# Fifteen small transfers move from SyncE's issue queue to ScalarE's in a two-block transformer kernel

## The reference

```
mod = silu(c) @ w_ada + b_ada                 # 2048 -> 12288, six parts of 2048
h   = rms_norm(x, g_attn_pre) * (1 + scale_a) + shift_a
proj = h @ w_in                               # 2048 -> 5456
... rope with positions; lam = exp(sum(lambda_q1*lambda_k1)) - exp(sum(lambda_q2*lambda_k2)) + lam_init
... differential attention, indexed sparse attention, @ w_o, gated feed-forward (w_gate, w_up, w_down)
... second block: rms_norm(x, pre_norm_g_2), @ w_in_2, latent attention with rope(positions_2),
    a gated convolution with conv_w_2, @ w_o_mla_2, @ w_o_conv_2, @ w_out_2
```

## Time and profile before

| what | value |
|---|---|
| median of 3 runs | 2428.31 us (2427.94 to 2430.77) |
| profiled execution, its own time | 2428.22 us |
| its span | 2426.9 us |
| PE busy / weight loads | 94% / 77% of the span |
| DVE, ACT busy | 58%, 44% |
| mean granted clock of PE | 0.978 of full |
| moved by the transfers | 505.69 MB, mean 208 GB/s |

### The profile page before, as it was taken

The page is one execution under the profiler, slowest core; times in us unless marked ns, Lnnn a source line. Parts: engine busy times, 40 slices in busy tenths (PEclk is TensorE's granted clock), DMA queues, the critical chain, the costliest instruction groups (busy, mean ns, idle before and its releaser), DMA issues.

```text
span 2426.9 us, 26309 instructions
## 1 busy us (share of the span) xinstructions
PE 2291.2 (94%) x10768; PEld 1861.1 (77%) x10768; DVE 1399.5 (58%) x1903; ACT 1062.3 (44%) x1469; POOL 0.7 (0%) x5
## 2 busy tenths in 40 slices
PE   4898989798999999999999999999999999999998
PEld 2676667676878888888887878788888888888886
DVE  1459898686666464454555555454544554554554
ACT  2333534444434444444444555555444444444443
POOL 0000000000000000000000000000000000000000
PEclk7999999899999999999999999999999999999999
DMA  7888678484776575556554644444555556556553
GB/s 296 333 314 306 216 262 285 153 306 166 247 273 243 192 259 191 191 191 191 191 189 143 210 157 154 153 152 152 185 196 192 188 184 197 183 186 194 187 190 139
DMA packets 255455, 505.69 MB, mean 208 GB/s; under 512 B 9077, under 2 KB 19662, under 8 KB 254182
## 3 DMA queue, kind: packets, MB, share of 16 engines
q1 hardware_dynamic: 255334, 504.00, 61.6%
HBM read 499.77 MB, written 4.19 MB: 208 GB/s over the span
## 4 chain that ended last, share of the span: by engine, by line
PE 82%; DVE 10%; ACT 3%; DMA 3%; issue 2%; SPq 0%; DVEq 0%; ACTq 0%
PE bank L566 26%; PE bank L568 25%; PE bank L567 25%; DVE wlo L1643 3%; DVE acc L1626 2%; PE bank L582 2%; DMA raw<-in_w_in_dram 2%; ACT whi L1033 1%; PE bank L650 1%; DMA raw<-in_w_ada_dram 1%; PE bank L520 1%; PE bank L590 1%; DVE x L1695 0%; ACT Ex_b L1162 0%; PE bank L673 0%
## 5 line engine op out<-in xcount | busy, mean ns | idle before, releaser
L1643 DVE TENSOR_TENSOR wlo<-raw,whi 128x1024 fp32r<-128x1024 f32 (+2 forms) x760 | 910.5, 1205 | 887.6 <-ACT whi L1033 887.1
L1033 ACT ACTIVATE whi<-raw 128x1024 fp32r<-128x1024 f32 (+2 forms) x760 | 790.1, 1044 | 1035.2 <-PE bank L568 949.1
L566 PE MATMUL bank<-whi,Ahi 128*128 128x512 f32 (+2 forms) x2304 | 912.5, 396 | 37.8 <-DVE wlo L1643 21.2
L567 PE MATMUL bank<-wlo,Ahi 128*128 128x512 f32 (+2 forms) x2304 | 897.0, 389 | 0.0
L568 PE MATMUL bank<-whi,Alo 128*128 128x512 f32 (+2 forms) x2304 | 896.6, 389 | 0.0
L566 PEld LDWEIGHTS bank<-whi,Ahi 128*128 128x128 f32 x2304 | 438.1, 190 | 141.1 <-DVE wlo L1643 31.3
L568 PEld LDWEIGHTS bank<-whi,Alo 128*128 128x128 f32 x2304 | 437.7, 190 | 90.3
L567 PEld LDWEIGHTS bank<-wlo,Ahi 128*128 128x128 f32 x2304 | 438.5, 190 | 83.2
L1626 DVE SCALAR_TENSOR_TENSOR acc<-raw,cs,acc 128x512 f32<-128x512 f32 x224 | 153.4, 746 | 0.0
L566 PE MATMUL bank<-whi,Fhi 128*128 128x512 f32 x352 | 137.7, 391 | 0.0
L568 PE MATMUL bank<-whi,Flo 128*128 128x512 f32 x352 | 137.0, 389 | 0.0
(11 more groups left out here) (291 smaller groups left out, 1345.2 us busy)
## 6 DMA issues: line engine op xcount, KB each, us to landing
raw<-in_w_in_dram SPq DMA_DIRECT2D x156, 1024.0 KB, 5.0
raw<-in_w_ada_dram SPq DMA_DIRECT2D x96, 1024.0 KB, 5.3
raw<-in_w_gate_dram SPq DMA_DIRECT2D x44, 1024.0 KB, 5.1
raw<-in_w_up_dram SPq DMA_DIRECT2D x44, 1024.0 KB, 5.1
raw<-in_w_down_dram SPq DMA_DIRECT2D x44, 1024.0 KB, 5.0
raw<-in_w_o_dram SPq DMA_DIRECT2D x16, 1024.0 KB, 5.2
raw<-in_w_o_mla_dram SPq DMA_DIRECT2D x16, 1024.0 KB, 4.9
raw<-in_w_o_conv_dram SPq DMA_DIRECT2D x16, 1024.0 KB, 4.9
```

The source lines that it names most:

```text
L566: pe.matmul(o, a_hi, w_hi, start=beg, stop=False)
L567: pe.matmul(o, a_hi, w_lo, start=False, stop=False)
L1033: act.activation(m.whi[:, i % NHL, :, 0:n], m.raw[:, c % NRAW, 2 * h:2 * h + 2, 0:n], ACT.Copy).then_inc(m.s_hi, 1)
L1643: dve.tensor_tensor(m.wlo[:, i % NHL, :, 0:n], m.raw[:, c % NRAW, 2 * h:2 * h + 2, 0:n], m.whi[:, i % NHL, :, 0:n].bitcast(F32), ALU.subtr ...
```

## The change

Fifteen transfers leave SP's stream and go into ACT's. Nine of them (eight to `rows`, one to `brows`) stand at the head of ACT's stream, before the first table load. The other six (lambda four times, positions twice) stand in ACT's stream behind the sigmoid and ahead of the squares of x. Their sizes, targets and semaphores stay. On SP the constants are now followed at once by chunks 0 and 1, x, and the chunks from 2 on without anything between chunks 4 and 5.

```
+    A = m.A
+    for r0, n, src in ((R_C, 16, A["c"][0]), (R_G1, 16, A["g_attn_pre"][0]), (R_G2, 16, A["g_ffn_pre"][0]),
+                       (R_G3, 16, A["pre_norm_g_2"]), (R_QA, 4, A["q_a_norm_g_2"]),
+                       (R_KVA, 4, A["kv_a_norm_g_2"]), (R_SUB, 1, A["g_diff_sub"][0])):
+        act.dma_start(m.rows[r0:r0 + n, :], src.rearrange("(r n) -> r n", n=P)).then_inc(m.s_rows, 16)
+    act.dma_start(m.rows[R_CW:R_CW + 48, :], A["conv_w_2"].rearrange("k (r n) -> (k r) n", n=P)).then_inc(m.s_rows, 16)
+    act.dma_start(m.brows[:, :], A["b_ada"].rearrange("a (g n) -> (a g) n", n=P)).then_inc(m.s_brows, 16)
     for b in (4, 5):
         k.use(b)
     need.wait_ge(m.freed[4], 1)
     act.activation(m.sig[:, :], m.cols[:, R_C:R_C + 16], ACT.Sigmoid).then_inc(m.s_sig, 1)
+    for i, name in enumerate(("lambda_q1", "lambda_k1", "lambda_q2", "lambda_k2")):
+        act.dma_start(m.lraw[:, i, :], A[name][0:1, :].broadcast_to([P, 64])).then_inc(m.s_lamin, 16)
+    for i, name in enumerate(("positions", "positions_2")):
+        act.dma_start(m.pos[:, 2 * i:2 * i + 2], A[name].rearrange("a (t p) -> p (a t)", p=P),
+                      allow_slow_non_contiguous=True).then_inc(m.s_pos, 16)
     need.wait_ge(m.s_eps, 1)
...
     sp.dma_start(m.const[:, :], A["consts"]).then_inc(m.s_const, 16)
-    for r0, n, src in ((R_C, 16, A["c"][0]), (R_G1, 16, A["g_attn_pre"][0]), (R_G2, 16, A["g_ffn_pre"][0]),
...
-        sp.dma_start(m.rows[r0:r0 + n, :], src.rearrange("(r n) -> r n", n=P)).then_inc(m.s_rows, 16)
-    sp.dma_start(m.rows[R_CW:R_CW + 48, :], A["conv_w_2"].rearrange("k (r n) -> (k r) n", n=P)).then_inc(m.s_rows, 16)
-    sp.dma_start(m.brows[:, :], A["b_ada"].rearrange("a (g n) -> (a g) n", n=P)).then_inc(m.s_brows, 16)
     for c in range(2):
         load_chunk(c)
     for tb in range(2):
         sp.dma_start(x[:, tb, :], A["x"][0, tb * P:tb * P + P, :]).then_inc(m.s_x[tb], 16)
     for c in range(2, NRAW):
         load_chunk(c)
-    for i, name in enumerate(("positions", "positions_2")):
-        sp.dma_start(m.pos[:, 2 * i:2 * i + 2], A[name].rearrange("a (t p) -> p (a t)", p=P),
-                     allow_slow_non_contiguous=True).then_inc(m.s_pos, 16)
-    for i, name in enumerate(("lambda_q1", "lambda_k1", "lambda_q2", "lambda_k2")):
-        sp.dma_start(m.lraw[:, i, :], A[name][0:1, :].broadcast_to([P, 64])).then_inc(m.s_lamin, 16)
```

More of the change, by code:

```diff
@@ L2446, in sync_program @@
     sp.dma_start(m.const[:, :], A["consts"]).then_inc(m.s_const, 16)
-    for r0, n, src in ((R_C, 16, A["c"][0]), (R_G1, 16, A["g_attn_pre"][0]), (R_G2, 16, A["g_ffn_pre"][0]),
-                       (R_G3, 16, A["pre_norm_g_2"]), (R_QA, 4, A["q_a_norm_g_2"]),
-                       (R_KVA, 4, A["kv_a_norm_g_2"]), (R_SUB, 1, A["g_diff_sub"][0])):
-        sp.dma_start(m.rows[r0:r0 + n, :], src.rearrange("(r n) -> r n", n=P)).then_inc(m.s_rows, 16)
-    sp.dma_start(m.rows[R_CW:R_CW + 48, :], A["conv_w_2"].rearrange("k (r n) -> (k r) n", n=P)).then_inc(m.s_rows, 16)
-    sp.dma_start(m.brows[:, :], A["b_ada"].rearrange("a (g n) -> (a g) n", n=P)).then_inc(m.s_brows, 16)
     for c in range(2):
```

## The result

The changed kernel takes 2424.7 us (median of 12 runs, 2421.83 to 2425.88) against 2428.31 us for the kernel before beside it (12 runs, 2425.74 to 2430.77). The ratio is 0.9982 with a 95% interval of 0.9974 to 0.9991, so it is faster by 2.2 to 6.3 us. The forecast was 2418.5 us, 9.8 us faster. The medians differ by 3.6 us, which is less than the 4.9 us that the prediction took as the least that can be told from no change. The profiled execution took 2423.14 us with a span of 2421.8 us, 5.1 us shorter than before.

What follows compares the result with a forecast made beforehand. The prediction took the first 42 us as bound by the weights' arrival, with every shift reaching the end. 3.67 + 6.96 - 0.8 = 9.8 us off 2428.22 us gave 2418.4, forecast as 2418.5 us, range 2414.0 to 2425.0 us.

Steps and rivals of the forecast that it cites:

- What the six still cost: Moved transfers' small pieces still pass the 16 shared transfer engines: 0.6 us, with 0.2 us for the nine, 0.8 us.
- The upper bound of this very term: The six hold the transfer engines as long from ACT's queue as they do now from SP's: 6.96 us.
- The likeliest case's own range: Range of the forecast case itself, chance 0.72: 2414.5 to 2422.5 us around 2418.5 us.
- 3 us of clock: Half clock granted to PE as w_in products start may fall differently: counted 0, range 3 us each side.
- the hole counted in bytes: Low-end price of the gap between chunks 4 and 5, from lost flow: 4.1 us instead of 6.96 us.
- The head: Start of SP's stream: without the nine issues chunk 0 is issued and lands 3.67 us earlier.
- The hole: Between chunks 4 and 5: without the six, chunk 5 follows by 2.55 us, not 9.51 us, 6.96 us less.
- ACT's side: Issuing the fifteen on ACT costs 0: the nine end about 4.4 us, the six at 13.3 us, `cs` about 7 us.
- The shift reaches the end: After the early flow: the first w_in product's shift is the end's, since the rest hangs on its own events.
- A: Early flow: small pieces hold the engines wherever issued, so only 3.7 us are won, 2424.6 us; chance 0.14.
- B: Early flow: large transfers starve the small ones, `cs` comes at 22.9 us, gain 5.4 us, 2422.9 us; chance 0.07.
- C: ACT's six issues behind the sigmoid are held up to 6.35 us each, `diag` comes late, 2439.5 us; chance 0.04.

Runs made afterwards that it cites:

- six late: Against the changed kernel, SP issues the six ahead of chunk 13 and the nine stay on ACT: 2419.02 us, ratio 0.9961.
- six only: Against the kernel before, only the six move to ACT behind the sigmoid and the nine stay on SP: 2425.88 us, ratio 0.9989.
- six late, nothing on ACT: Against the kernel before, SP issues the six ahead of chunk 13 instead of behind chunk 4: 2423.38 us, ratio 0.9984.
- six behind chunk 13: Against the changed kernel, SP issues the six behind chunk 13 and the nine stay on ACT: 2420.43 us, ratio 0.9969.

## Why the prediction was wrong

**The step that failed** is "What the six still cost", the term of 0.8 us (0.6 for the six, 0.2 for the nine). The six cost 3.8 us (43.21 against 39.41) to 5.0 us (43.72 against 38.74), 4.6 us where they alone were moved, and the nine 0.3 us (chunk 4 at 21.87 and 21.86, where 25.27 - 3.67 is 21.60) to 1.3 us (22.87 in the kernel with the six ahead of chunk 13). Together they made chunk 4 late by 26.69 - 21.60 = 5.1 us. With 5.1 in place of 0.8 the sum is 3.67 + 6.96 - 5.1 = 5.5 us, which is the lead measured at the first w_in product.

The term was read from the DMA share: busy time less what the GB/s explain. This counts how long pieces are recorded as moving, 15 to 18 ns for each of lambda's. It says nothing of the time between the pieces, in which the flow is held. I read the share of 0.17 as "the engines are free for another queue". The runs show that they were so only in part. With a second queue beside it the hole shrank from 7.0 to 4 or 5 us; it did not vanish. Why a slow read in one queue slows the pieces of the other is not shown by any of these runs. By the transfer records of the changed kernel SP's pieces of 2 KB take 96 ns on the mean from 13 to 22 us, against 84 ns in undisturbed flow, and the DMA share falls to 0.82; so a part is slower pieces and the rest is idle engines. The upper bound of this very term, 6.96 us, was in the prediction, and the truth lies between the bounds, nearer to the upper one. The high end of the range, 2425.0 us, held the median of 2424.7 us, but the value was taken at the wrong end. The likeliest case's own range, 2414.5 to 2422.5 us, does not follow from the two terms named for it either: 3 us of clock on each side, and 2.9 us more above for the hole counted in bytes, give 2415.5 to 2424.4 us.

**The head** (3.67 us): right. Chunk 4 comes 3.4 us earlier where only the nine move.

**The hole** (6.96 us): right. Without the six in the early flow the first product comes 7.1 us earlier with the head left as it was. Counting by landings and not by bytes (4.1 us) was right too.

**ACT's side**: right that it costs little, wrong about `cs`. The nine issues took it to 5.0 us. The six took 2.8 us, from 9.61 to 12.43 us, and the first square of x began at 12.53 us. `cs` came at 11.8 us and not at 7 us, beyond the 10 us from which the prediction had expected a cost. That cost little at most: the kernels with the six late have the same lateness (the transpose of `rows` at 10.00 and 8.89 us) and reach 39.41 and 38.74 us, 0.6 to 1.3 us from the 38.1 us that both gains leave. Whether these 0.6 to 1.3 us come from the late `cs` or from the nine in the flow isn't shown.

**The shift reaches the end**: right on the average, not in each case. In the profiled executions 5.5 us at the first product became 5.1 us in the span, but the medians differ by 3.6 us only, within an interval of 2.2 to 6.3 us. In the other kernels the lead at the first product and the gain of the median are 2.3 and 3.5 us (six only), 9.3 and 10.3 us (six late), 7.1 and 3.8 us (six late, nothing on ACT), 10.0 and 8.4 us (six behind chunk 13). The clock moves the time by as much, and the prediction had counted it as 0 with 3 us on each side. At the same place of the program (windows, columns as above; the kernel before, then the changed one) half clock lasted 10.2 us before and 13.7 us after:

```profile
563.20:573.40 10.20, 3.78 (x16) 3.49 (x16) 6.23 (x15) 5.86 (x18) 0.00 (x0) 0.50 0.01 3
```

```profile
555.50:569.20 13.70, 7.61 (x25) 6.54 (x26) 8.62 (x17) 6.48 (x17) 0.00 (x0) 0.51 0.00 0
```

PE did 7.6 us of work there at about half clock, against 3.8 us before. DVE's low halves on either side show the lead falling there: ahead of it 557.53 us before and 548.87 us after, 8.7 us; behind it 582.91 and 575.95 us, 7.0 us. The rest went near 1450 us, where the changed kernel was granted 0.52 from 1446.4 to 1449.8 us. So the lead rose from 5.5 to 8.7 us and fell again, and that it ended at 5.1 us, so near to where it began, is chance. What the difference between 5.1 and 3.6 us is made of stays open.

**The rivals.** A (the small pieces hold the engines wherever they are issued) was nearest, 2424.6 us against 2424.7, but its mechanism is only partly right: 4 to 5 of the 7.0 us were kept, and by the traces the lead is 5.5 and not 3.7 us, so that its number fits the median is luck. Its own sign, under 200 GB/s for several us between 8 and 20 us, came for one slice only (144 GB/s). The sentence of the Trainium skill behind A ("DMA: Bandwidth & Descriptors", "Issuing engines are not separate DMA queues"), that only issue time is saved, is nearer to the runs than my reading of the shares. What it leaves out is the 2.3 us that moving the six alone gave. B came about in a mild form: the `rows` transfers took 4.7 us in place of 1.8 us beside the large ones, and `cs` was late by 4.7 us, at little or no cost. C did not happen: one issue on ACT took at most 0.74 us in the profile of the changed kernel.

## What to carry to other kernels

A transfer that is slow for its size (single words, or one source row read for all 128 partitions) should leave the stretch in which the weights' arrival sets the pace. Another issue queue beside that stretch recovered only part of it here: the other queue gave 2.3 us and the later place 7.1 us. To price a hole, read the distance between the landings on either side, and don't take a low busy share of the transfer engines as room for another queue. Where a change moves a few us out of 2400, read the lead from one stretch of the profile to tell causes apart, and leave the gain itself to the medians: here a lead of 7.1 us in one stretch came with 3.8 us in the medians.

## What the runs showed of the hardware

- Reading the same 256 bytes for 128 partitions, four times, held a queue 5.0 us longer than reading 4 x 128 distinct pieces of the same size (the hole is 7.0 against 2.0 us; one run, with the source in another tensor). The four transfers move 128 KB, which at 410 GB/s would be 0.3 us. The pieces themselves are recorded with 15 to 18 ns each in both cases.
- Small transfers beside a full flow on another queue landed late but were not starved. From its issue to its landing b_ada's 48 KB took 1.8 us before and 6.3 us after.
- A slow read on ACT's queue slowed the large transfers on SP's queue: together they moved 267 GB/s at a DMA share of 0.82, against 405 at 1.05 right behind it. In one queue the same reads had left 233 GB/s at 0.64.
- Two profiled executions of one kernel (the kernel before) were 3.1 us apart at 557 us and 0.4 us apart at the end.
